# The scan of an RWKV-7 layer: token-pair products over all four quadrants of TensorE in turn

## What is computed

```python
def rwkv7_scan(r, w, k, v, a_vec, b_vec, s0):
    def step(S, inp):
        rt, wt, kt, vt, at, bt = inp
        sa = jnp.einsum('bhij,bhj->bhi', S, at)
        S = S * wt[:, :, None, :] + sa[..., None] * bt[:, :, None, :] + vt[..., None] * kt[:, :, None, :]
        return S, jnp.einsum('bhij,bhj->bhi', S, rt)
```

## Time and profile before

| | |
|---|---|
| median of 3 runs | 3102.15 us |
| span of the profiled execution, first to last instruction | 3092.7 us |
| median less span (what lies around the span) | 9.45 us |
| PE busy | 2704.7 us, 87% |
| DVE busy | 1464.7 us, 47% |
| scan block of the first layer | about 852 to 1003 us |
| scan block of the second layer | about 2368 to 2520 us |

### The profile page before, as it was taken

How to read it: one execution, slowest core, us unless ns; L and a number is a source line. 1 busy time by engine, 2 the same in 40 slices (tenths; PEclk the granted TensorE clock), 3 DMA queues, 4 the chain that set the end, 5 groups by cost and what they waited for, 6 DMA issues and landing times. The chain is left out here.

```text
span 3092.7 us, 53427 instructions
## 1 busy us (share of the span) xinstructions
PE 2704.7 (87%) x22862; PEld 2389.3 (77%) x22862; DVE 1464.7 (47%) x2073; ACT 820.6 (27%) x1218; POOL 162.0 (5%) x102
## 2 busy tenths in 40 slices
PE   5988888997698898999969879888967979799997
PEld 3777775886588698999958768567946859799997
DVE  3344346434655665334351541744366566633443
ACT  1221214223311323333222111332241114333331
POOL 0011110300000000000000210112000000000000
PEclk9997999996599799999979879999956989899999
DMA  6222345721000341222341330656010015322232
GB/s 257 98 59 58 113 134 185 228 72 52 14 3 3 126 177 66 98 82 83 137 148 35 86 120 23 219 183 200 16 52 15 3 44 178 110 83 82 83 110 109
DMA packets 216310, 305.16 MB, mean 99 GB/s; under 512 B 28021, under 2 KB 97191, under 8 KB 214786
## 3 DMA queue, kind: packets, MB, share of 16 engines
q1 hardware_dynamic: 216066, 301.67, 29.0%
HBM read 266.49 MB, written 35.14 MB: 98 GB/s over the span
## 5 line engine op out<-in xcount | busy, mean ns | idle before, releaser
L379 PE MATMUL pb<-h_high,f_high 128*128 128x260 f32 x1984 | 401.5, 284 | 4.9 <-DVEq L2619 4.9
L379 PE MATMUL pb<-h_low,f_high 128*128 128x260 f32 x1984 | 398.6, 282 | 0.0
L379 PE MATMUL pb<-h_high,f_low 128*128 128x260 f32 x1920 | 387.7, 283 | 0.0
L554 DVE TENSOR_TENSOR w_low<-ring,w_high 128x2048 fp32r<-128x2048 f32 x66 | 151.3, 2293 | 405.7 <-ACT w_high L546 404.3
L379 PEld LDWEIGHTS pb<-h_high,f_high 128*128 128x128 f32 x1984 | 306.5, 188 | 5.3 <-issue 5.3
L379 PEld LDWEIGHTS pb<-h_low,f_high 128*128 128x128 f32 x1984 | 307.6, 189 | 0.0
L554 DVE TENSOR_TENSOR f_low<-ring,f_high 128x2048 fp32r<-128x2048 f32 x60 | 137.6, 2293 | 339.1 <-ACT h_high L548 214.2
L379 PEld LDWEIGHTS pb<-h_high,f_low 128*128 128x128 f32 x1920 | 294.5, 188 | 0.0
L757 POOL TENSOR_TENSOR g_low<-yT,g_high 128x512 fp32r<-128x512 f32 x96 | 159.9, 1670 | 1978.0 <-ACT g_high L753 1978.0
L379 PE MATMUL pb<-w_high,h_high 128*128 128x512 f32 x560 | 224.9, 402 | 20.9 <-DVEq L558 11.7
L379 PE MATMUL pb<-w_low,h_high 128*128 128x512 f32 x560 | 224.2, 400 | 0.0
(11 more groups left out here) (362 smaller groups left out, 4620.2 us busy)
## 6 DMA issues: line engine op xcount, KB each, us to landing
ring<-in_w_ff_dram SPq DMA_DIRECT2D x32, 2048.0 KB, 7.8
ring<-in_w_in_dram SPq DMA_DIRECT2D x20, 2048.0 KB, 9.1
ring<-in_w_ada_dram SPq DMA_DIRECT2D x18, 2048.0 KB, 8.1
yT<-in_w_in_dram SPq DMA_DIRECT2D x96, 256.0 KB, 3.6
arena<-in_w_ada_dram SPq DMA_DIRECT2D x9, 2048.0 KB
gate_spill_dram<-yT SPq DMA_DIRECT2D x48, 260.0 KB, 4.0
arena<-gate_spill_dram SPq DMA_DIRECT2D x12, 1040.0 KB, 5.4
arena<-in_cache_k_diff_dram SPq DMA_DIRECT2D x32, 256.0 KB, 3.1
```

Of the source, the lines that this page charges most:

```text
L379: return PE.matmul(out, lhsT, rhs, start=start, stop=stop, skip_group_check=True)
L554: t = V.tensor_tensor(ws[n % 2][1], ring[slot][:, u * 2048:(u + 1) * 2048], ws[n % 2][0].bitcast(F32), sub)
```

## The change

`products` loses its parameter g. It now makes both halves in one call, and for each pair of heads it visits the quadrants in the order (0,0), (1,1), (0,1), (1,0). The operands, the banks and the number of matmuls stay. In the chunk's own work the whole of the next tile's ba or br now stands ahead of the wait for `rhs_copied`; the half that stood behind the multiplication by the inverse is gone from there.

```diff
-                    def products(left, right, m, bank, g):
-
-                        gs = slice(g * 64, (g + 1) * 64)
+                    def products(left, right, m, bank):
+
                         for hp in range(HP):
-                            for cc in range(2):
+                            for g, cc in ((0, 0), (1, 1), (0, 1), (1, 0)):
+                                gs = slice(g * 64, (g + 1) * 64)
                                 tok = slice(m * P + cc * CH, m * P + (cc + 1) * CH)
                                 t = mm(at(pb[bank + g], 0, HP, CH)[lower[cc], hp], left[gs, hp, tok], right[gs, hp, tok])
                         return t
...
-                    products(z1, z2, 0, 4, 0)
-                    products(z1, z2, 0, 4, 1).then_inc(ba_made, 1)
-                    products(z1, r_, 0, 6, 0)
-                    products(z1, r_, 0, 6, 1).then_inc(br_made, 1)
+                    products(z1, z2, 0, 4).then_inc(ba_made, 1)
+                    products(z1, r_, 0, 6).then_inc(br_made, 1)
...
-                        products(k_, z2, m, 4, 0)
-                        products(k_, z2, m, 4, 1).then_inc(ka_made, 1)
+                        products(k_, z2, m, 4).then_inc(ka_made, 1)
...
-                                products(k_, r_, m, 6, 0)
-                                products(k_, r_, m, 6, 1).then_inc(kr_made, 1)
+                                products(k_, r_, m, 6).then_inc(kr_made, 1)
...
                             if m + 1 < MT:
-                                products(z1, (z2, r_)[cc], m + 1, 4 + 2 * cc, 0)
+                                products(z1, (z2, r_)[cc], m + 1, 4 + 2 * cc).then_inc((ba_made, br_made)[cc], 1)
                             pe.wait_ge(rhs_copied, n + 1)
                             for h, hp, g, hs, gs in heads:
                                 t = mm(pb[1][r, hs], xt[r, g, hp], rhs1[r, hs])
                             t.then_inc(u_made, 1)
-                            if m + 1 < MT:
-                                products(z1, (z2, r_)[cc], m + 1, 4 + 2 * cc, 1).then_inc((ba_made, br_made)[cc], 1)
```

## The result

The change makes the kernel faster by about a quarter of a percent. Over 22 runs of each the median fell from 3098.13 us to 3090.76 us; the ratio is 0.9974 with a 95% interval of 0.9964 to 0.9983. Of 3098 us that ratio makes 8.1 us, between 5.3 and 11.2; the two medians differ by 7.4 us.

What follows compares the result with a forecast made beforehand. PE and DVE taking turns bound the scans, each product bound by its quadrant. Gains of 3.5 (ka, kr), 3.1 (next tile's products) and 0.8 us (clock) sum to 7.4 us, giving 3094.8 us, range 3090.5 to 3103.

Steps and rivals of the forecast that it cites:

- What bounds the scan: In the two scans, about 153 us each, PE and DVE take turns; time saved there is saved by the kernel.
- Four quadrants at 58 ns each: In the products, each quadrant takes 58 ns a pair; all four in turn make 32 pairs in 0.47 us.
- Both rivals on the speed of the stream: Product pairs: 20 ns each, gain 2.8 us, chance 0.13; or 29 ns each, 3.6 us slower, chance 0.07.
- ka and kr: Start of each of 8 tiles: ka 0.35 us earlier plus kr's end, 0.44 us a tile, 3.5 us in all.
- kr's tail: Behind kr, its half 1 holds quadrant (1,1) when the next product wants it, for some 0.09 us.
- The next tile's products: In the chunks, 6 times: gain 0.12 us in the first, 0.39 in the second; 0.51 a tile, 3.1 in all.
- charge of 0.07 us for the wait: Second chunk: work in quadrant (1,1) now ahead of the wait for the copy was charged 0.07 us.
- Tile 0's products: Tile 0's ba and br: gain 0, hidden by DVE's split of y and memset; without cover under 0.6 us a layer.
- Clock: Low stretches and tile 0 at 1.2 GHz: longer pairs save more, at most 2.2 us extra, 0.8 us counted.
- The level, and so the time: Whole kernel: span 3085.3 us plus the 9.4 us between span and median gives 3094.8 us.
- Clock luck as a rival: Tile starts: two more low stretches give 3097.8 us, chance 0.12; two fewer 3091.8 us, chance 0.13.
- The case of 25 ns: Matmul starts in the products never closer than about 25 ns: 3102.7 us, no change, chance 0.05.

Runs made afterwards that it cites:

- quads_only: Kernel before with four quadrants in turn, the next tile's products keeping their old place and two halves: ratio 0.9997 to the kernel before, full-clock tile 35.48 us.
- copies_first: Changed kernel with ACT's two copies of xm ahead of its scaling of v by the bonus: single run, last tile 33.01 us, both scans 284.63 us.
- ahead_only: Changed kernel with each call doing half 0, then half 1 as before, next tile's products all ahead of the wait: ratio 0.9988 to the kernel before.
- before_filled: Kernel before plus 24 useless identity matmuls in PE's idle ahead of a tile: ratio 0.9975 to the kernel before, both scans 288.47 us.
- fill_again: Changed kernel plus 24 useless identity matmuls in PE's idle ahead of a tile, second measurement: ratio 0.9941 to the kernel before, both scans 282.36 us.
- fill_idle: Changed kernel plus 24 useless identity matmuls in PE's idle ahead of a tile, first measurement: ratio 0.9950 to the kernel before, both scans 283.12 us.
- diagonals: Changed kernel with each call using two quadrants at a time, (0,0) with (1,1), then (0,1) with (1,0): single run, full-clock tile 35.41 us.
- ka_early: Changed kernel with the next tile's ka made at the end of the second chunk: ratio 0.9974 to the kernel before, full-clock tile 34.64 us.
- br_late: Changed kernel with the next tile's br made behind the second chunk's output: ratio 0.9972 to the kernel before, full-clock tile 34.90 us.

## Why the prediction was right or wrong, point by point

**What bounds the scan.** Right. The tile at full clock came out at 34.91 us, 34.9 in the text. Outside the scans the stretches moved by +1.7 us ahead of them, -4.3 us between them and +2.0 us behind, which happens to add up to -0.6; the one between them varies by 10 us among kernels that are the same there.

**Four quadrants at 58 ns each.** Right: 32 loads in 0.60 us, 15 ns apart on average. Both rivals on the speed of the stream (20 and 29 ns a pair) are refuted. The trace of the kernel before could have told it: where the halves of ka overlap, single loads start in fours within 15 ns (933.638, .640, .647 and .653), and the next four 57 ns later. By this the trace does not agree, in this kernel, with the floor of about 25 ns from start to start that the Trainium skill states (page "TensorE: Matmul & The Clock Gate", section "Wait — 56ns, not 53.3ns?").

**ka and kr.** Forecast 0.44 us a tile, measured 0.37 (quads_only). The ka term was 0.35 and came to 0.26. After the change the 32 matmuls start within 0.52 us (2405.59 to 2406.11) and not 0.47, since the first one starts with its load and the later ones 0.06 us behind theirs, and the mask follows the last record's end (2406.33) by 0.08 us instead of 0.05. kr's tail was 0.11 instead of 0.09. One reading was wrong but did no harm: "that mask is not waiting for PE". DVE's work ahead of kr's mask ends at 935.79, and the mask starts at 935.90:

```profile
935.05 0.74 DVE L2163 TENSOR_TENSOR yT<-pb,cst 128x256 f32<-128x256 f32 x2
```

DVE's instructions otherwise start some 0.08 us ahead of the end of the one before, so it did wait, nearly 0.2 us. It has the time: behind kr's masks it waits for PE again. In the last tile the term was 0.27, not 0.44: there ACT's copies, not ka, release the first level, which copies_first shows, and what is left is kr, whose mask comes 0.25 us earlier. I had not looked at the last tile by itself.

**The next tile's products.** Forecast 0.51 us a tile, measured 34.91 against 35.48, 0.57: 0.12 in the first chunk, as forecast, and 0.45 in the second. Of the charge of 0.07 us for the wait there 0.01 was found. The experiments add why the two edits belong together: the place alone brings 0.32, the order alone 0.37, both 0.94. The 0.25 us left over is the delay of u in ahead_only, 0.12 + 0.14, which four quadrants take away.

**Tile 0's products.** Gain 0, as forecast: PE's 64 pairs take 1.98 instead of 2.60 us, and DVE's first mask still comes right behind its memset, 2.63 us after PE's start.

**Clock.** I added 0.8 us because pairs last longer at 1.2 GHz. That was wrong in its mechanism. Tile 0, which runs at the low clock for its first 6.4 us, went from 37.88 us (before_filled) to 37.00 (fill_again), 0.88 us, no more than a full-clock tile. In both kernels the clock rises 6.3 to 6.4 us behind the tile's start; time that is won ahead of that moment is won at half speed, so I take it that this gives back what the long pairs gain. Without it the sum was 6.6 us, and the scans with the clock's luck removed show 6.1. The other 0.96 us of the 7.07 us between the two profiles came from where the low stretches fell: one at the very start of a tile costs 0.9 us (35.80 against 34.91), one in its third to sixth microsecond 1.5, one in the last tile 0.3 before (34.92 against 34.64) and nothing after.

**The level, and so the time: the step that failed.** "With the 9.4 us between span and median the time is 3094.8 us." I took the difference of span and median for something that lies around the span. The profiled run after the change took 3086.87 us with a span of 3085.1: 1.8 us lie around, and in every later run of the kernel before with a span on record it is 1.7 to 1.9 us. So the profiled run before took about 3094.5 us, and the rest of the 9.4, 7.6 us, was the spread of the runs. Of three runs none was below 3101; of 22, half were below 3098.13, and they go from 3088.91 to 3109.15. Against that median my time was a change of 3.3 us where 8.1 were measured (7.4 by the medians). The working had 7.4. Part of the spread lies in the stretch between the two scans, whose instructions are the same in all kernels but lasted from 1363.7 us (fill_idle) to 1373.9 us (diagonals). The granted clock has a share in it: of this stretch 287 us ran at 1.2 GHz in fill_idle and 301 in diagonals, 284 after the change and 308 before, and over the 14 profiles that time and the length have a correlation of 0.67. In the 22 runs of the change time and mean clock (0.895 to 0.904) have one of -0.77, in three groups of runs of the kernel before only about -0.4. So the clock is a part of the cause, and the rest is open.

**Clock luck as a rival.** That the clock moves the time was right, and it is more than I gave it: in quads_only and ahead_only it ate the whole gain of a shorter tile in the scans. How it would do so was not: the number of low stretches was four in every kernel that left the idle alone, and what moved was their place and length. PE's idle did not grow either, it was 1.92 us before and after. And "at 1.5 us each" held for three of the four; the one in the last tile cost 0.3.

**The case of 25 ns.** Its time was a small slip: on the line between -2.8 us at 20 ns and +3.6 at 29 ns a pair, 25 ns is +0.8, so 3102.9 us and not 3102.7. Nothing else hung on it.

## What to carry to other kernels

In this kernel matmuls of 64x64 went four at a time, 15 ns a pair instead of 29, once the stream visited all four quadrants in turn; two calls that each use half of the array could be merged at no cost, and the block of such work then fitted in front of a wait that it overran otherwise. Work that can be done early belongs where PE would stand idle, for its own time and because the idle was followed by a low clock here. And a time is forecast as a difference to many runs: three runs can all lie on one side.

## What the runs showed that I had not expected

- Useless matmuls in an idle of 1.9 us gain time: 24 of them, 6 times, gave 3.2 to 4.0 us in the scans (286.36 to 283.12 and 282.36 us), because the stretches of 3.4 us at a clock of 0.50 behind the idle are gone. With 0.9 us of real work in that idle they were gone too, with 0.5 us of it not all.
- A low stretch in the last tile can last 6.8 us (quads_only, ahead_only, ka_early, br_late) where another lasts 3.4; what tells them apart was not tested.
- Products that stand ahead of an urgent one in the stream can delay it by much less than their own length: in ahead_only the product with the inverse was 0.12 us late in the first chunk and 0.14 in the second, not 0.4. It is not that they lie in other quadrants, since in the second chunk they do not; the cause is open.
